# Twenty of 24 gate tiles as 2x2 block products, their tanh kept in DRAM, all gates ahead of all projections

## The reference

```python
h = rms_norm(x, pre_norm_w)
p = h @ w_in                                   # among its columns: p_gate, 3 x 1024
ys = stack([y_a, y_b, y_c])                    # each 1024 tokens x 512
proj = einsum('nbsc,ncd->nbsd', ys, w_branch)  # three times 512 -> 1024
gates = sigmoid(p_gate.reshape(b, s, 3, 1024))
merged = einsum('bsnd,nbsd->bsd', gates, proj)
x = x + rms_norm(merged @ w_out, post_norm_w)
# second block: attention and retention, then
h = h + (silu(m @ w_gate) * (m @ w_up)) @ w_down      # 1024 -> 2816 -> 1024
```

## Time and profile before

| | us |
|---|---|
| median of 3 runs | 2356.12 (2351.52 to 2357.4) |
| the profiled execution, time | 2354.78 |
| its span, first to last instruction | 2352.6 |
| TensorE busy | 2302.5 (98%) |
| VectorE busy | 1294.5 (55%) |
| ScalarE busy | 742.4 (32%) |
| GpSimd busy | 495.4 (21%) |
| mean granted TensorE clock | 0.991 |

### The profile page before, as it was taken

How to read it: one execution, slowest core, us unless ns; L and a number is a source line. 1 busy time by engine, 2 the same in 40 slices (tenths; PEclk the granted TensorE clock), 3 DMA queues, 4 the chain that set the end, 5 groups by cost and what they waited for, 6 DMA issues and landing times.

```text
span 2352.6 us, 30971 instructions
## 1 busy us (share of the span) xinstructions
PE 2302.5 (98%) x12632; PEld 1893.9 (81%) x12632; DVE 1294.5 (55%) x2171; ACT 742.4 (32%) x1240; POOL 495.4 (21%) x346
## 2 busy tenths in 40 slices
PE   8999999999999999999999999999899999999999
PEld 7788788877878888888887777778688888888887
DVE  4677777778832313244458776654766666621223
ACT  5323333333331211232244444432233233232210
POOL 3312223123100012022122212200432222241200
PEclk9999999999999999999999999999899999999999
...
DMA packets 239036, 183.37 MB, mean 78 GB/s; under 512 B 43312, under 2 KB 217008, under 8 KB 238896
## 3 DMA queue, kind: packets, MB, share of 16 engines
...
...
## 4 chain that ended last, share of the span: by engine, by line
PE 86%; DVE 10%; issue 1%; POOL 1%; ACT 1%; DMA 1%; SPq 0%; ACTq 0%; DVEq 0%
PE PS L120 83%; PE PS L123 3%; DVE qx L129 1%; DVE Ntmp L129 1%; DVE Nn L129 1%; DVE T1f L129 1%; DVE qr L129 1%; POOL sm L129 0%; DVE smx L2066 0%; DVE ST L137 0%; DVE Yt L137 0%; DMA g_row<-in_pre_norm_w_dram 0%; DVE sm L1878 0%; DVE Wlo L129 0%; DVE Yt L129 0%
## 5 line engine op out<-in xcount | busy, mean ns | idle before, releaser
L120 PE MATMUL PS<-Hhi,Whi 128*128 128x512 f32 (+1 forms) x1680 | 530.4, 391 | 6.8 <-ACT tg L126 3.9
L120 PE MATMUL PS<-Hhi,Wlo 128*128 128x512 f32 (+1 forms) x1680 | 530.7, 391 | 0.0
L120 PE MATMUL PS<-Hlo,Whi 128*128 128x512 f32 (+1 forms) x1680 | 530.6, 391 | 0.0
L126 ACT ACTIVATE Whi<-Wraw 128x512 fp32r<-128x512 f32 (+1 forms) x262 | 163.5, 624 | 760.7 <-PE PS L120 757.0
L120 PEld LDWEIGHTS PS<-Hhi,Whi 128*128 128x128 f32 x1680 | 311.0, 189 | 69.1 <-ACT tg L126 4.3
L120 PEld LDWEIGHTS PS<-Hlo,Whi 128*128 128x128 f32 x1680 | 311.1, 189 | 63.3 <-issue 5.4
L120 PEld LDWEIGHTS PS<-Hhi,Wlo 128*128 128x128 f32 x1680 | 310.8, 189 | 63.4 <-issue 4.3
L129 DVE TENSOR_TENSOR Wlo<-Wraw,Whi 128x512 fp32r<-128x512 f32 (+1 forms) x180 | 134.3, 746 | 372.4 <-ACT Whi L126 371.9
L129 POOL TENSOR_TENSOR Wlo<-Wraw,Whi 128x512 fp32r<-128x512 f32 x82 | 127.6, 1558 | 389.7 <-ACT Whi L126 389.5
L120 PE MATMUL PS<-YMhi,Wlo 128*128 128x512 f32 (+1 forms) x328 | 108.8, 384 | 10.9 <-DVE Wlo L129 10.9
L129 DVE TENSOR_TENSOR Ntmp<-Nn 32x30 f32<-32x30 f32 (+14 forms) x240 | 90.3, 376 | 37.5 <-DMA Nn<-scr_ns 31.4
...
## 6 DMA issues: line engine op xcount, KB each, us to landing
Wraw<-in_w_in_dram SPq DMA_DIRECT2D x166, 256.0 KB, 2.8
scr_fb<-fb SPq DMA_DIRECT2D x22, 512.0 KB, 3.1
fin<-scr_fb SPq DMA_DIRECT2D x22, 512.0 KB, 3.5
wA<-in_w_gate_dram SPq DMA_DIRECT2D x36, 256.0 KB, 3.2
wA<-in_w_up_dram SPq DMA_DIRECT2D x36, 256.0 KB, 3.6
Wraw<-in_w_down_dram SPq DMA_DIRECT2D x32, 256.0 KB, 2.8
Wraw<-in_w_branch_dram SPq DMA_DIRECT2D x24, 256.0 KB, 2.8
yst<-scr_y SPq DMA_DIRECT2D x12, 512.0 KB, 3.6
```

The costliest lines, as they stand in the source:

```text
L120: return self.h.matmul(out, lhsT, rhs, start=start, stop=stop, skip_group_check=True)
L126: return self.h.activation(out, in_, func, **kw)
```

## The change

The number of plain gate tiles falls to four, n = 1, d = 0 to 3. The other 20 are taken as ten pairs of neighbouring tiles, each a 2x2 block product over the two halves of k and of the tokens, with the same functions as the feed-forward: these now take a block `("g", i)` or `("f", f)` and read from `K.bp["g"]` or `K.bp["f"]`. For gates the order of products is A11, S2, S3, S1, S4, A12, A22. T1's parts are written over B12 (tokens' second half, first four k-tiles of `Hhi`, `Hlo`), which only plain tiles read; T2, T3, T4 and the weights' sources lie in the region that `region_free` guards, partly where `Yhi`, `Ylo`, `yst` and `zst` follow.

The order of the stage becomes: 4 plain gate tiles, 10 blocks, and then all 24 projections in one run. The tanh of a gate goes to one of four staging tiles `stg` and is stored to DRAM (`scr_g`, 512 KB a tile); it is loaded into `tg[d]` ahead of its projection, and VectorE's product waits for that load. The branch output n = 2 has its own place, `Hhi[:, 4:8]`, free after the last block. In the product by tokens that follows, the first five k-tiles now run with k outermost over the first three token tiles.

All order strings and `PICKS` are new. In VectorE's, `T` and `S` steps for the gates stand in a row after the last `w` before the gates: `T l T l T2 S T S T S2 T S2 T S T2`, with the steps of S being S1, S2, lo S2, S3, lo S3, S4, lo S4. On GpSimd it is `T2 S T S3 T`. ScalarE casts, in this order: A11, (a tanh), S2, S3, S1, T2, S4, A12, T4, A22, T3, the next block's A11, (a tanh), T1. At the entry of the feed-forward VectorE has `T3 w S w2 S T w ...` where it had `T4 S T w2 S w S T w ...`, and GpSimd `T S T2 S4 T` where it had `T2 S T S T`. SyncE waits for S4's sum, too, before the next block's weights.

```diff
+PLAIN_G, PLAIN_F = [(1, d) for d in range(4)], (0, 1, 20, 21)
+PAIRS_G = [(1, 4), (1, 6)] + [(n, d) for n in (2, 0) for d in (0, 2, 4, 6)]
+BLOCKS_G = [("g", i) for i in range(len(PAIRS_G))]
+BLOCKS_F = [("f", f) for f in range(2, 20)]
+BLOCKS = BLOCKS_G + BLOCKS_F
+LAST = {"g": BLOCKS_G[-1], "f": BLOCKS_F[-1]}
+PRODUCTS = {"g": (("A11", "B11", "a"), ("S2", "T2", "b"), ("S3", "T3", "d"), ("S1", "T1", "c"), ("S4", "B22", "e"),
+                  ("A12", "B21", "a"), ("A22", "T4", "d")),
+            "f": (("A11", "B11", "a"), ("S4", "B22", "e"), ("S2", "T2", "b"), ("S1", "T1", "c"), ("S3", "T3", "d"),
+                  ("A12", "B21", "a"), ("A22", "T4", "d"))}
+TILES_G = PLAIN_G + [(n, d + i) for n, d in PAIRS_G for i in range(2)]
+N_BACK = {"g": 2 * len(ORDER1) + 2 * len(PLAIN_G)}
...
+        G = self.bp["g"] = Blocks("g", self.Hhi, self.Hlo)
+        mg = Bump(nc, R1, R2)
+        G.comb["T1"] = mg("gT1f", [128, 4, HT])
+        G.blocks["T1"] = G.blocks["B12"]
+        G.slots = self.weight_slots("g", mg)
+        mg.at += 4096
+        for n_, o in (("T4", mg.at), ("T2", R2), ("T3", R2 + 16384)):
+            G.blocks[n_] = (at("g" + n_ + "hi", [128, 4, HT], F32R, offset=o)[:], at("g" + n_ + "lo", [128, 4, HT], F32R, offset=o + 8192)[:])
+            G.comb[n_] = at("g" + n_ + "f", [128, 4, HT], F32, offset=o + 8192)
...
+        self.stg = [mg(f"stg{i}", [128, T]) for i in range(4)]
+        mg = Bump(nc, R2 + 32768, R2 + 49152)
+        G.wsrc = {n_: mg("gw" + n_, [128, 4, 128]) for n_ in WSRC}
...
             yield from dense([tile], K.Hhi, K.Hlo, h_ready)
-        for n, kind, d in ORDER_BR:
-            if kind == "g":
-                yield from dense([([4, 4], ("g", n, d), [S.gate_act.at((n, d))])], K.Hhi, K.Hlo, h_ready)
-            else:
-                yield from dense([([4], ("p", n, d), [S.proj_dve.at(("dp", n, d))])], K.Yhi, K.Ylo,
+        for n, d in PLAIN_G:
+            yield from dense([([4, 4], ("g", n, d), [S.gate_act.at((n, d))])], K.Hhi, K.Hlo, h_ready)
+        for b in BLOCKS_G:
+            yield from block_products(b)
+        for n in (1, 2, 0):
+            for d in range(8):
+                yield from dense([([4], ("p", n, d), [S.proj_dve.at(("dp", n, d))])], *K.Y[n],
...
-        yield from by_token([(i, k) for i in range(3) for k in range(7)] + [(i, 7) for i in range(3)]
+        yield from by_token([(i, k) for k in range(5) for i in range(3)] + [(i, k) for i in range(3) for k in range(5, 8)]
...
+        for t, (n, d) in enumerate(PLAIN_G):
+            act.wait_ge(*S.dense_pe.at(("tile", ("g", n, d))))
+            act.act(K.stg[t][:], banks.of(("dp", ("g", n, d))), ACT.Tanh, scale=0.5).then_inc(*S.gate_act.tick((n, d)))
+            yield
+        x1 = K.bp["g"].sums[0]
+        for b, (n, d) in zip(BLOCKS_G, PAIRS_G):
+            t = TILES_G.index((n, d))
+            one, two = K.stg[t % 4], K.stg[(t + 1) % 4]
...
+            act.wait_ge(*S.ffn_dve.at(("u2", b)))
+            act.act(two[:, HT:], two[:, HT:], ACT.Tanh, scale=0.5).then_inc(*S.gate_act.tick())
+            yield
+            act.wait_ge(*S.ffn_dve.at(("g2", b)))
+            act.act(one[:, HT:], one[:, HT:], ACT.Tanh, scale=0.5).then_inc(*S.gate_act.tick())
+            yield
+            act.wait_ge(*S.dense_pe.at(("prod", "A12", b)))
+            act.wait_ge(*K.gate_stored(t - 4))
+            act.act(one[:, 0:HT], banks.of(("st", "a", b)), ACT.Tanh, scale=0.5).then_inc(*S.gate_act.tick(("a", b), (n, d)))
+            yield
+            act.wait_ge(*S.ffn_dve.at(("u1", b)))
+            act.act(two[:, 0:HT], two[:, 0:HT], ACT.Tanh, scale=0.5).then_inc(*S.gate_act.tick((n, d + 1)))
+            yield
...
+            for name in ("T2", "T4", "T3", "T1") if kind == "g" else ("T1", "T2", "T4", "T3"):
+                act.wait_ge(*(S.comb_pool if name == "T3" else S.comb_dve).at((kind, name)))
+                if name in ("T1", "T2"):
+                    act.wait_ge(*S.comb_dve.at((kind, {"T1": "T2", "T2": "T4"}[name])))
+                if (kind, name) == ("g", "T1"):
+                    act.wait_ge(*S.dense_pe.at(("tile", ("g",) + PLAIN_G[-1])))
+                act.act(P.blocks[name][0], P.comb[name][:], ACT.Copy).then_inc(*S.comb_act.tick((kind, name)))
...
-            dve.wait_ge(*S.gate_act.at((n, d)))
+            dve.wait_ge(*(S.fbi0_dma, S.fbi1_dma, S.fbi2_dma)[r % 3].at(("g", r)))
...
+    def block_sums(b, x1, x6, v, u2, *before):
+        dve.wait_ge(*(S.gate_act if b[0] == "g" else S.ffn_act).at(("x1", b)))
+        dve.wait_ge(*S.dense_pe.at(("prod", "S2", b)))
+        if b != BLOCKS_G[0]:
+            dve.wait_ge(*S.ffn_dve.last())
+        dve.tt(x6[:], banks.of(("st", "b", b)), x1[:], ALU.add).then_inc(*S.ffn_dve.tick(("x6", b)))
+        yield
...
+        for b, (n, d) in zip(BLOCKS_G, PAIRS_G):
+            t = TILES_G.index((n, d))
+            one, two = K.stg[t % 4], K.stg[(t + 1) % 4]
+            yield from block_sums(b, x1, x6, v, lambda: two[:, HT:], K.gate_stored(t - 3))
+            dve.wait_ge(*S.dense_pe.at(("prod", "S4", b)))
+            dve.wait_ge(*K.gate_stored(t - 4))
+            dve.tt(one[:, HT:], banks.of(("st", "e", b)), v[:], ALU.add).then_inc(*S.ffn_dve.tick(("g2", b)))
+            yield
+            dve.wait_ge(*S.dense_pe.at(("prod", "A22", b)))
+            dve.tt(two[:, 0:HT], banks.of(("st", "d", b)), x6[:], ALU.add).then_inc(*S.ffn_dve.tick(("u1", b)))
+            yield
...
+            for step in ("S1", "S2", "lo S2", "S3", "lo S3", "S4", "lo S4") if kind == "g" else (
+                    "S1", "S2", "S4", "lo S4", "lo S2", "S3", "lo S3"):
...
+            for name in ("T2", "T4", "T1") if kind == "g" else ("T2", "T1", "T4"):
...
+                if (n, k) == (1, 0):
+                    sp.wait_ge(*K.sum_lo("S4", LAST["g"]))
+                    sp.wait_ge(*K.sum_lo("A22", LAST["g"]))
...
+                sp.wait_ge(*S.sum_dve.at(("S3", (kind, b[1] - 1))))
+                sp.wait_ge(*S.sum_dve.at(("S4", (kind, b[1] - 1))))
+                sp.wait_ge(*K.sum_lo("A11", (kind, b[1] - 1)))
...
+        for t, (n, d) in enumerate(TILES_G):
+            sp.wait_ge(*S.gate_act.at((n, d)))
+            if t > 1:
+                sp.wait_ge(*K.gate_stored(t - 2))
+            sp.dma(D["scr_g"][t], K.stg[t % 4][:]).then_inc(*(S.fbo0_dma, S.fbo1_dma)[t % 2].tick(("g", t), by=16))
+            yield
...
+        fbi = (S.fbi0_dma, S.fbi1_dma, S.fbi2_dma)
+        for r, (n, d) in enumerate([(n, d) for n in (1, 2, 0) for d in range(8)]):
+            t = TILES_G.index((n, d))
+            if r > 2:
+                sp.wait_ge(*fbi[r % 3].at(("g", r - 3)))
+            if r == 0:
+                sp.wait_ge(*S.comb_dve.at(("g", "lo", "T1")))
+            elif r == 1:
+                sp.wait_ge(*S.dense_pe.at(("prod", "S2", LAST["g"])))
+            elif n == 1 and d > 2:
+                sp.wait_ge(*K.gate_stored(22))
+                sp.wait_ge(*K.gate_stored(23))
+            elif n != 1:
+                sp.wait_ge(*(S.proj_dve.at(("m", 1, d)) if n == 2 else S.proj_pool.at(d)))
+            sp.wait_ge(*K.gate_stored(t))
+            sp.dma(K.tg[d][:], D["scr_g"][t]).then_inc(*fbi[r % 3].tick(("g", r), by=16))
+            yield
+        sp.wait_ge(*S.ffn_dve.at(("fb", 19)))
         for f in range(22):
...
     "dve":
...
-        "ip3ip3fpf2if2ififi16pf2i2f7s2fs2fi4ci6cis2is2csisici4sci6ci4cificfg2ig2i2gigi4gfi3fgi16fi5fw2f2ws4wf"
-        "cfcs4c2wc3wcg6wg2wlbwblwb2tw3tw3tw3tw3tw3twtwtwb2wbwbwbw3tw3tw3tw3tw3tw3twtwtwb3wbwb2wbw13twtmtwtmwt"
-        "3wmt2mwt2mwt2mwt2mwtmn5h2n3h2n3h2n2hnhnh2n3h2n3h2n3h2r5w4kwk2wk2wk4wkwok2owr2krkrwrkr3kwx2r2xr3y2rxo"
...
-        "z3k2zwyz2vx3y3x2z2yzyxd2zyzd3zdwvwAwdAdwAd2AdAdA3n3hnh3n3hnh3n2h2n2h2n2h2n2h2T4STw2SwSTwS3uTuTST2u3S"
-        "3uS3u2Su6S3uS3u2Su6S3uS3u2Su6S3uS3u2Su6S3uS3u2Su6S3uS3u2Su6S3uS3u2Su6S3uS3u2Su6S3uS3u2Su6S3uS3u2Su6S"
...
+        "2fs2fi2ci5cis2i2scs3ci4csi3ci5ci2fcg2fg2i2gigi4gi3fgi2fi16fi4fi2wi3wf2w2s2fs2fcs2cs2cwc4wcg6wg2wTlTl"
+        "T2STSTS2TS2TST2SuS5u3Su2S2uS2uS2uSu2S2uS2uS2uSu2S2uS2uS2uSu2S2uS2uS2uSu2S2uS2uS2uSu2S2uS2uS2uSu2S2uS"
...
+        "xy3wz2ydzykdzyzdzwkd2kvdw2AwdAdwAd2AdAdA3n3hnh3n3hnh3n2h2n2h2n2h2n2h2T3wSw2STwSuS3TSu2T2uT2STSuSuS3u"
+        "Su7SuS2uS3uSu5SuS2uS3u2Su6SuS2uS3uSu5SuS2uS3u2Su6SuS2uS3uSu5SuS2uS3u2Su6SuS2uS3uSu5SuS2uS3u2Su6SuS2u"
...
     "pool":
-        "w3q5wq3w4pwpw6p2w11gwp2w6pwgpw8gw2pwpw4gwpwpw11pgwpw7gp2w9gw3gt8m8n16xyzk3okorxkyzkxoyzxyzoxryzkxkoy"
-        "kzxyorzxyk2ozxykozrxkykzxyn8T2STSTS70u22",
+        "w3q5wq3w4p2w6pwpw10gwpwpw6gp2w8gw4p2w4gw2p2w9gw2pwpw5pgpw11gw3gT2STS3TS36t8m8n16xyzk3okoxrykzxkyozxy"
+        "zxoyrkzkxyokzxyorzxyk2zxyokzxkyorzxykn8TST2S4TS67u22",
```

More of the change, by code:

```diff
@@ L246 @@
 N_LO_POOL = 2 * len(ORDER1)
[L247 to L255, removed]
+PLAIN_G, PLAIN_F = [(1, d) for d in range(4)], (0, 1, 20, 21)
[10 more added lines that the diff above has]
+N_BACK = {"g": 2 * len(ORDER1) + 2 * len(PLAIN_G)}
+N_RG_LAST = N_BACK["g"] + 24 + 2 * (len(ORDER_2) - 2)
```

(33 more changed lines are left out.)

438 lines of the change are left out of this document (227 added, 211 removed).

## The result

| | before | after |
|---|---|---|
| median of 4 runs each, us | 2354.66 (2351.52 to 2357.4) | 2327.74 (2326.72 to 2329.55) |
| profiled execution, time; span | 2354.78; 2352.6 | 2329.55; 2327.7 |
| TensorE busy; matmuls | 2302.5; 12632 | 2274.7; 12512 |

The ratio is 0.9887 with an interval of 0.987 to 0.9904, 27 us faster. The forecast was 2339 with a range of 2326 to 2350; the narrower range that its main case was given, 2329 to 2348, was missed by 1 us. The profiled executions differ by 24.9 us; the sum of the prediction had 17.2 there (27.2 - 20 + 10).

The account below looks back on a forecast made before the run. TensorE was taken to bound the kernel, busy 2302.5 of 2352.6 us. From 2354.8, -27.2 (matmuls) + 20 (gates' start) - 10 (feed-forward entry) gave 2337.6, as a median about 2339 us, range 2326 to 2350.

Parts of the forecast that it names:

- main case: The whole change: a median near 2339 us, range 2329 to 2348, chance 0.63.
- Matmuls: Gates: ten pairs of tiles as blocks, 84 matmuls instead of 96 each, save 120 matmuls, 27.2 us.
- The start of the gates: After the last scr_y store: T2 and T3 come late through turn-taking of VectorE and GpSimd; loss 20 us.
- The first rival: Gates' start: the token combinations are in time, so nothing is lost there; median 2319 us, chance 0.12.
- Steady blocks: Later gate blocks: VectorE's work and the added tanh stores stay covered; cost 0, ends 0 and +3 us.
- projections: Run of 24 projections: the added gate tile loads stay hidden; cost 0, ends -1 and +4 us.
- The third rival: Projections become bound by transfers, 6.3 us a tile instead of 5.4; median 2359 us, slower, chance 0.08.
- The feed-forward entry: Entry to feed-forward: TensorE's wait for Wlo falls from 10.9 to 2.0 us, lo T3 costs 1.5; saves 10 us.
- The second rival: Feed-forward entry keeps its loss because lo T3 takes the place of Wlo; median 2349 us, chance 0.17.
- Other orders: First 688 us and attention stage, reordered with equal work: 0, ends -4 and +4 us.

Follow-up runs that it names:

- g_not3: The changed kernel without T3 for the gates (GpSimd forms none, ScalarE casts none, the product S3·T3 takes T2's tiles); 2310.75 us, ratio 0.9813.
- g_t3dve: The changed kernel with T3 of the gates formed by VectorE instead of GpSimd, in a hand-written order; 2320.81 us, ratio 0.9849.
- b_ffn: The kernel before with only the feed-forward's order strings and picks from the changed kernel; 2354.57 us, ratio 0.9999.
- a_fold: The changed kernel with the feed-forward's orders of the kernel before, gates and attention as in the changed one; 2330.28 us, ratio 0.9889.
- gf_t3dve: As g_t3dve, with T3 of the feed-forward's first matrix formed by VectorE too; 2312.66 us, ratio 0.9814.

## Why the prediction was right, and where it was off

**Matmuls, -27.2.** The count fell by 120, and the pitch is unchanged: the chain of the new kernel after the start is

```profile
735.82 186.78 PE PS L120 x816
```

0.2289 us each with the slow first ones in it, against 0.2269 and 0.2279.

**The start of the gates, +20.** The stage gained 9.4 us, 10.0 from the last `scr_y` store (686.95 where it was at 686.37), so 17.2 were lost of the 27.2. T2's low half was forecast for 726.4 and came at 726.3; T3's for 736 and came at 735.7. The waits, 9.9 and 3.9, are those of the forecast, and the matmuls between and behind them ran at the lower clock. The term is 2 to 3 too large. S3·T3 started 16.5 us late and not 17.4 (735.8 against 719.3, the 716.6 at which TensorE stopped and 12 matmuls), and of the slow clock's loss 2.4 us lay in the product S2·T2, in time in which TensorE would have waited for T3 anyway; only the 1.6 behind it count. And the sum left out that the kernel before had a wait of its own in this stage, for a branch output, which the new kernel hasn't:

```profile
PE PS L120 <- DVE Ylo L129: 1.2, 1, 1.2
```

16.5 + 1.6 - 1.2 is 16.9, near the 17.2.

That turn-taking with GpSimd makes T2 late is shown by g_not3, where VectorE has the same steps in the same order and is 13 us sooner. The Trainium skill has this as a rule ("SBUF — State Buffer", "Who interferes with whom"): a VectorE instruction with two SBUF inputs and a GpSimd instruction that reads SBUF shut each other out for a whole instruction. The trace agrees: the 128x4 instructions of VectorE ended at 696.0, when GpSimd's first T3f had ended at 695.8. For T3 it is shown less cleanly: g_t3dve, which has T3's low half 16.5 us sooner, changed the orders of VectorE and ScalarE too. In the new kernel ScalarE casts T3 only behind S4, A12, T4 and A22 (cast at 727.5, T3 formed by 712.9), and whether a better place of that cast alone would remove the 3.9 us was not tried.

The first rival (2319, combinations in time) is refuted: pieces of 6.6 us and both waits came. Its count of 23 us to lo T2 is nearly met in g_not3, by 24.3.

**Steady blocks, 0, and projections, 0.** Both hold: 122.00 of 122 us busy, and 130.90 of 131. The third rival is refuted beyond the change's own load: at 306 GB/s nothing waits. A gate tile takes 5.3 us to land there, not the 3.5 of the row of before, but it is asked for ahead, and so the sum of two latencies in series that the rival was priced by never occurs (no wait of TensorE is listed in that run). The first projection began at 922.4, forecast 924.

**The feed-forward entry, -10.** This step failed in size. The first part came as forecast: `Wlo` made TensorE wait 1.4 us instead of 10.9, the clock held (1.00 in 1627 to 1690), and the plain tiles gained 11.1. But the first block was given 1.5 us of loss and took 7.7. The waits in the new kernel:

```profile
1691.56 0.47 PE L120 MATMUL PS<-T1hi,Whi 128*128 128x512 f32 x1 [0.31 <-DVE T1lo L129]
...
1695.98 0.47 PE L120 MATMUL PS<-T3hi,Whi 128*128 128x512 f32 x1 [1.44 <-POOL T3lo L129]
...
1704.71 0.52 PE L120 MATMUL PS<-T4hi,Whi 128*128 128x512 f32 x1 [3.04 <-DVE xu L129]
```

T3's low half cost 1.44, as forecast (1.5). What was not counted is behind it, on VectorE:

```profile
1691.33 5.05 DVE L129 TENSOR_TENSOR wS<-wA,wA 128x512 f32<-128x512 f32 x1
1696.31 2.28 DVE L129 TENSOR_TENSOR T4lo<-T4f,T4hi 128x2048 fp32r<-128x2048 f32 x1
...
1703.98 0.68 DVE L129 TENSOR_TENSOR xu<-PS,xv 128x512 f32<-128x512 f32 x1
```

A 512-column sum for the next block was held for 5 us by GpSimd's lo T3, and the drain of a finished product, `xu`, stood behind it and T4's low half; TensorE needed that bank for the last product. The lower clock came on top: behind the 3.04 us it was 0.55 between 1704.7 and 1708.2, and the 12 matmuls of that product took 4.4 us instead of 2.7. The three waits and this are 6.5 of the 7.7. I had followed the operands of the first block and not the results that free its banks. The net 3.8 us of the profiled executions don't show in the medians (b_ffn 0.9999; a_fold 0.9889 beside 0.9887), so the worth of this part is put between 0 and 4 here, and no run fixes it more closely. That turn-taking holds this block up too is supported by gf_t3dve, where T3's wait goes and `xu`'s shrinks to 1.8; its orders were written anew as well. The second rival said this part would give nothing, for lo T3's sake; as to size it came near, but by way of `xu`.

**Other orders, 0 (-4 to +4).** This step failed too, beyond its own bound, and it is what makes the forecast too high. The stages before 688 are where they were. The attention stage was 11.5 us shorter. The last 60 us of that stage, first of the kernel before, then of the new one:

```profile
1500.00:1560.00 60.00, 54.39 (x318) 42.79 (x318) 32.79 (x70) 26.75 (x54) 3.46 (x4) 0.89 0.22 53
```

```profile
1480.00:1540.00 60.00, 59.22 (x395) 48.24 (x394) 38.04 (x58) 23.51 (x41) 8.61 (x6) 0.97 0.27 67
```

Idle time of 5.6 us against 0.8, and a mean clock of 0.89 against 0.97. With two levels, 1.2 and 2.4 GHz, 0.89 means 13 of the 60 us at the lower one, 6.6 us of matmul time; 0.97 means 1.8 us. Together some 10 us of the 11.5. TensorE's waits of 0.6 to 2.1 us there in the kernel before:

```profile
1518.92 0.97 PE L123 MATMUL PS<-cst,smx 128*128 128x128 f32 x6 [2.06 <-DVE smx L133]
...
1520.64 2.83 PE L120 MATMUL PS<-smx,vtk 128*64 128x128 f32 x24 [0.74 <-DVE smx L140]
...
1532.81 1.22 PE L120 MATMUL PS<-Hhi,Whi 128*128 128x512 f32 x2 [1.35 <-DVE qb L137]
```

In the last softmax blocks TensorE waited there for one step of VectorE after another. In the new kernel one wait of 0.8 us is left in that stretch. The row for the whole stage had shown 10.8 us of gaps and a clock of 0.98, which is 7 us: together the prize was some 18, and the bound of 4 was set without working that out. Which of the moved steps brings the gain isn't settled, since the strings of all engines were changed as one; that it comes from these orders alone is (404.2 and 404.3 us with the old ones whatever the gates, 391.4 to 394.4 with the new).

In sum: forecast -27.2 + 20 - 10 + 0 = -17.2; measured -10.0 (gates, with the half microsecond at their start given back) + 0.6 - 0.2 - 11.5 - 3.8 = -24.9. The forecast gave the feed-forward 6 us too much, attention 11.5 too little and the gates 3 too little. The mechanism at the gates was right and is what the runs show; that the time lies within the range is in part luck, since errors of opposite sign met. With the 10 us forecast for the feed-forward and all else as measured, it would have been some 2321, below the range.
